# Placing the weight slabs of a four-layer trunk in the SBUF ring by a fixed order of use

## The reference, cut to what matters

```
for i in range(4):
    mod = silu(cond) @ w_ada[i] + b_ada[i]                 # 1024 x 6144: shift, scale, gate, twice
    h = rmsnorm(x) * (1 + sc1) + sh1
    y = (hyena, gla, fnet, pool)[i](h)                     # w_in, w_out / wq, wk, wv, wg, wo / fn / pool
    x = x + g1 * y
    h = rmsnorm(x) * (1 + sc2) + sh2
    # each token: the best group of four experts, in it the best two
    hid = silu(h @ w1[e]) * (h @ w3[e])                    # 1024 x 512 each
    x = x + g2 * sum_e combine[e] * (hid @ w2[e])          # 512 x 1024
y = rmsnorm(x)
```

## Time and profile before

| | before |
|---|---|
| median of 3 runs | 1425.84 us (1425.6 to 1426.71) |
| the profiled execution, whole | 1427.96 us |
| its span on the core | 1425.8 us |
| PE busy | 1277.1 us (90% of the span) |
| VectorE busy | 478.4 us (34%) |
| ScalarE busy | 278.1 us (20%) |
| read from HBM | 551.08 MB, 388 GB/s over the span |
| mean granted clock of TensorE | 0.955 |

### The profile page before, as it was taken

The page is one execution under the profiler, slowest core; times in us unless marked ns, Lnnn a source line. Parts: engine busy times, 40 slices in busy tenths (PEclk is TensorE's granted clock), DMA queues, the critical chain, the costliest instruction groups (busy, mean ns, idle before and its releaser), DMA issues.

```text
span 1425.8 us, 17690 instructions
## 1 busy us (share of the span) xinstructions
PE 1277.1 (90%) x7052; PEld 713.4 (50%) x7052; DVE 478.4 (34%) x1127; ACT 278.1 (20%) x502; POOL 32.1 (2%) x30
## 2 busy tenths in 40 slices
PE   9999999999847999999999757999997589999846
PEld 5776585444313878775444324754443245444312
DVE  3777515111103987525112102151121045111103
ACT  3311024111103221333111004331111044111101
POOL 0001310000000000010000000100000000000000
PEclk9999999999969999999999978999999799999968
DMA  9997989999999987799999999798999996999994
GB/s 385 420 417 299 402 366 406 375 429 426 428 424 421 387 362 300 276 385 391 397 427 428 428 423 420 288 413 350 430 425 427 424 422 277 397 427 427 427 425 174
DMA packets 57962, 554.41 MB, mean 389 GB/s; under 512 B 6353, under 2 KB 8337, under 8 KB 9489
## 3 DMA queue, kind: packets, MB, share of 16 engines
q1 hardware_dynamic: 56096, 551.19, 93.5%
q10 hardware_dynamic: 1778, 2.01, 0.4%
HBM read 551.08 MB, written 2.10 MB: 388 GB/s over the span
## 4 chain that ended last, share of the span: by engine, by line
PE 78%; DMA 18%; DVE 2%; ACT 1%; issue 1%; POOL 0%; SPq 0%; DVEq 0%; ACTq 0%; POOLq 0%
PE bank L797 27%; DMA ring<-in_moe_w 18%; PE bank L737 14%; PE bank L821 9%; PE bank L697 4%; PE bank L756 3%; PE bank L774 3%; PE bank L580 2%; PE bank L566 2%; PE bank L711 2%; PE bank L1052 1%; PE bank L934 1%; PE bank L647 1%; PE bank L641 1%; PE bank L984 1%; PE bank L924 1%
## 5 line engine op out<-in xcount | busy, mean ns | idle before, releaser
L797 PE MATMUL bank<-ring,arena 128*32 128x512 f32 (+1 forms) x1024 | 185.6, 663 | 92.5 <-DMA ring<-in_moe_w 92.5
L797 PE MATMUL bank<-ring,hT 128*64 128x512 f32 x1024 | 225.5, 594 | 8.6 <-DMA ring<-in_moe_w 8.6
L1572 DVE TENSOR_TENSOR rows<-rows,bank 128x512 f32<-128x512 f32 x28 | 19.3, 688 | 481.3 <-PE bank L797 481.3
L821 PE MATMUL bank<-ring,arena 128*64 128x512 f32 (+1 forms) x768 | 150.7, 642 | 18.0 <-DMA ring<-in_moe_w 17.7
L797 PEld LDWEIGHTS bank<-ring,arena 128*32 128x32 f32 (+1 forms) x1024 | 56.2, 134 | 214.6 <-issue 213.5
L797 PEld LDWEIGHTS bank<-ring,hT 128*64 128x64 f32 x1024 | 75.3, 137 | 145.9 <-issue 144.7
L737 PE MATMUL bank<-hT,ring 128*128 128x256 f32 x512 | 113.5, 381 | 0.0
L1591 DVE SCALAR_TENSOR_TENSOR yv_rest<-bank,arena,yv_big 128x512 fp32r<-128x512 f32 x56 | 42.0, 751 | 202.0 <-ACT yv_big L1250 202.0
L737 PEld LDWEIGHTS bank<-hT,ring 128*128 128x128 f32 x512 | 96.3, 190 | 18.2 <-ACT arena L1333 3.4
L821 PEld LDWEIGHTS bank<-ring,arena 128*64 128x64 f32 (+1 forms) x768 | 46.5, 135 | 108.1 <-issue 108.1
L1250 ACT ACTIVATE yv_big<-bank,arena 128x512 fp32r<-128x512 f32 x56 | 38.5, 687 | 284.1 <-PE bank L821 284.1
(11 more groups left out here) (238 smaller groups left out, 1376.6 us busy)
## 6 DMA issues: line engine op xcount, KB each, us to landing
ring<-in_moe_w SPq DMA_DIRECT2D x144, 2048.0 KB, 20.5
ring<-in_w_ada SPq DMA_DIRECT2D x96, 1024.0 KB, 11.0
ring<-in_moe_w SPq DMA_DIRECT2D x64, 1024.0 KB, 13.5
arena<-in_moe_w SPq DMA_DIRECT2D x32, 1024.0 KB, 13.7
ring<-in_hy_w_in SPq DMA_DIRECT2D x12, 1024.0 KB, 26.7
ring<-in_hy_w_out SPq DMA_DIRECT2D x4, 1024.0 KB, 10.2
ring<-in_gla_w_v SPq DMA_DIRECT2D x4, 1024.0 KB, 10.2
ring<-in_gla_w_g SPq DMA_DIRECT2D x4, 1024.0 KB, 10.8
```

The source lines that it names most:

```text
L797: last = mm(bank[4 + kind][m * o:m * o + m, :], x[:, k, at:at + m], ws[o][:, kk, :], start=k == 0, stop=k == KD - 1)
L821: last = mm(bank[6 + h][m * o:m * o + m, :], hidT[:, f, m * o:m * o + m], ws[o][:, f, :], start=f == 0, stop=f == 3)
```

## The change

The stream keeps its order. The mark `cond_done` goes. The place of a piece is now chosen by `ring_places`: `use_order` gives each piece a fixed number that stands for the time at which it is used up, and a new piece takes the place whose last piece has the lowest number (the lower place where two are equal); a couple takes the two places, even and next, whose higher number is lowest. The further rounds take places 0 to 11 by their kind and quarter. The switch `TWO_EARLY` is on and is read in `use_order` alone.

```diff
--- before.py
+++ after.py
@@ -38,6 +38,7 @@
 RING = 14
 SLAB = 2048
 SLABS = 4
+TWO_EARLY = True
 ADAS = 3 * LAYERS
 COUPLES = PAIRS // 2
 HALF = D // 8 + 1
@@ -149,10 +150,10 @@
               + wk[1:] + ada(6, 4, 6) + wv[0:1] + ada(8, 0, 2) + wv[1:2] + ada(6, 6, 7) + ada(8, 2, 4) + wv[2:3]
               + ada(6, 7) + ada(8, 4, 6) + wv[3:] + ada(7, 0, 1) + ada(8, 6) + ada(7, 1, 2) + wg[0:1] + ada(7, 2, 4)
               + wg[1:2] + ada(7, 4, 6) + wg[2:3] + ada(7, 6, 7) + wg[3:] + ada(7, 7) + ada(9) + pieces("wo", 4)
-              + ada(10) + [("cond_done", 6)],
+              + ada(10),
               pieces("fn", 4) + ada(11),
               pieces("pool", 1)]
-    out, at, held = [], 0, None
+    out = []
     for i in range(LAYERS):
         experts = [("moe", i, p, kind, q) for p in range(QUAD) for kind in range(3) for q in ((0, 2, 1, 3) if p else range(SLABS))
                    if p or kind < 2]
@@ -160,23 +161,55 @@
                     for h in range(2)]
         experts += [("moe", i, p, 2, 2 * h + e) for h in range(2) for p in (QUAD, QUAD + 1) for e in range(2)]
         for what in before[i] + experts[0:2] + [("first", i)] + experts[2:] + [("further", i)]:
-            if what[0] in ("first", "further"):
-                out.append((what, None, None))
-                continue
-            if homed(what):
-                out.append((what, None, None))
-                continue
-            if what[0] == "cond_done":
-                held = None
-                continue
-            if at % RING == held:
-                at += 1
-            if in_halves(what) and not second_half(what):
-                at += at % 2
-            if what[0] == "cond":
-                held = at % RING
-            out.append((what, at % RING, at // RING))
-            at += 1
+            out.append(what)
+    return ring_places(out)
+
+
+def use_order(what):
+
+    name, c = what[0:2]
+    if name == "moe":
+        _, i, p, kind, q = what
+        return 1000 * i + 400 + 25.7 * min(p, QUAD) + 9 * kind + 3.5 * (q // 2 + 1) + (0 if p < QUAD or kind < 2 else 0)
+    if name == "ada":
+        n, k = c, what[2]
+        if n == 0:
+            return 10 + 3.5 * k
+        if n == 1:
+            return 53 + 10 * k
+        if n == 2:
+            return 75 + 14 * k if TWO_EARLY and k < 4 else 126 + 2.5 * k
+        if n in (3, 4, 5):
+            return (146, 162, 212)[n - 3] + 2.3 * k
+        if n == 6:
+            return 1000 + (20, 25, 30, 38, 52, 55, 62, 67)[k]
+        if n == 7:
+            return 1000 + (72, 77, 82, 86, 108, 113, 118, 128)[k]
+        if n == 8:
+            return 1000 + {0: 52, 1: 53, 2: 61, 3: 62, 4: 70, 5: 71, 6: 79, 7: 80}[k]
+        if n == 9:
+            return 1000 + (142, 147, 153, 154, 160, 161, 162, 163)[k]
+        return (1192 if n == 10 else 2040) + 1.8 * k
+    return {"w_in": 47 + 7 * c, "w_out": 190 + 7 * c, "cond": 1128, "wq": 1019 + 7 * c, "wk": 1038 + 7 * c,
+            "wv": 1052 + 7 * c + (2 * c if TWO_EARLY else 0), "wg": 1000 + (80, 111, 118, 140)[c % 4], "wo": 1168 + 7 * c,
+            "fn": 2018 + 7 * c, "pool": 3010}[name]
+
+
+def ring_places(order):
+
+    free, out = [-1.0] * RING, []
+    for n, what in enumerate(order):
+        if what[0] in ("first", "further") or homed(what):
+            out.append((what, None, None))
+            continue
+        if second_half(what):
+            slot = out[-1][1] + 1
+        elif in_halves(what):
+            slot = min(range(0, RING, 2), key=lambda m: (max(free[m:m + 2]), m))
+        else:
+            slot = min(range(RING), key=lambda m: (free[m], m))
+        free[slot] = use_order(what)
+        out.append((what, slot, None))
     return out
 
 
@@ -529,7 +562,7 @@
                         for kind in range(3):
                             sp.wait_ge(s("fb_" + USED[kind]), primed(2 * (2 * (b + c) + j)))
                             for q in range(SLABS):
-                                sp.dma_start(ring[where["moe", i, 1, kind, q][0]][:],
+                                sp.dma_start(ring[SLABS * kind + q][:],
                                              expert_slab(kind, q // 2, EXPERTS * i + PAIRS * (q % 2) + j + 2 * c)) \
                                     .then_inc(s(f"fb_full{kind}"), 16)
                 for kind in range(3):
@@ -899,7 +932,7 @@
 
                         def weights(kind, h):
                             pe.wait_ge(s(f"fb_full{kind}"), 16 * SLABS * (n + 1))
-                            return [ring[where["moe", i, 1, kind, 2 * h + e][0]].rearrange("p (k n) -> p k n", k=4)
+                            return [ring[SLABS * kind + 2 * h + e].rearrange("p (k n) -> p k n", k=4)
                                     for e in range(2)]
 
                         pe.wait_ge(s(pre + "hidT_ready"), primed(n))
```

## The result

The changed kernel takes 1434.13 us (median of 5 runs, 1432.15 to 1435.18), the kernel before beside it 1426.71. The ratio is 1.0047, 95% interval [1.0032, 1.0063]: slower by 4.6 to 9.0 us. The profiled execution is the run of 1435.18 us, with a span of 1433.0.

A forecast was written before the change was run, and what follows sets the result against it. The prediction took the kernel to be bound by moving its weights over DMA. Its terms, 0 + 0.9 + 4.0 + 2.9 = 7.8 us, took the 1425.8 us span and the median to 1433.6 us, range 1429.0 to 1439.5.

The forecast's parts named there:

- Layer 0: Term for layer 0: issues move by a microsecond or two inside a full queue, gap at 262 us unchanged; 0 us.
- Retention mixer: Term for layer 1's mixer: `wv` 3 waits for `wv` 0, VectorE's 3.51 us slack covers the lateness; 0 us.
- Layer 1: Term for layer 1's expert stage: third couple waits for unit 0, seventh lands late; +0.9 us, bounds 0 and 3.4.
- Layer 2: Term for layer 2: torn second couple waits for unit 0's first quarter, less the old gap; +4.0 us, bounds 2.0 and 6.9.
- estimate of 6.8 us and 3.2: Alternative for layer 2: second couple's transfer taking 6.8 us, not 7.6, making that term 3.2 us; not used in the sum.
- Layer 3: Term for layer 3: second couple waits for unit 0's first quarter, its transfer moving behind an idle stretch; +2.9 us, bounds 2.2 and 4.9.
- grow by about the sum: Sign of being right: PE's waits on the two expert lines grow by about the summed terms, 7.8 us.
- The start: Sign of being right: PE's expert waits begin in the fifth unit of layers 2 and 3 rather than the sixth.
- the forgiving gap: Rival, not slower: late couples caught up before the second unit's gap in layers 2 and 3; 1425.8 us, chance 0.08.
- the mixer's slack: Within rival slower by more (1438.6 us, chance 0.13): VectorE's 3.51 us in layer 1's mixer fails to cover held pieces, +2.6.

The follow-up runs named there:

- e4: Kernel before, with the w1 and w3 slabs of unit 1 loaded as single slabs in order of use, not as couples: 1416.31 us, ratio 0.9924.
- e10: Kernel before, places untouched, with `wv` 3 in the retention mixer waiting for the second `wv` piece: 1430.85 us, ratio 1.0031.
- e1: Changed kernel, but both halves of a couple count as given back when the second is, in all layers: 1427.63 us, ratio 1.0007.
- e2: Changed kernel, with both halves given back together for layer 1's couples alone, which mends layer 2: 1430.61 us, ratio 1.0027.
- e3: Changed kernel, with both halves given back together for layer 2's couples alone, which mends layer 3: 1431.26 us, ratio 1.0035.
- e12: The e1 kernel run again, beside e11 on the same chip: 1426.77 us, ratio 0.9996.
- e11: Second run of the e1 kernel with two slabs of unit 0 of layer 1 exchanging places: 1431.54 us, ratio 1.0035.
- e6: Kernel before, places untouched, with layer 2's second couple waiting for the first quarter of unit 0: 1430.85 us, ratio 1.0031.
- e7: Kernel before, places untouched, with layer 2's second couple waiting for the second quarter of unit 0: 1433.62 us, ratio 1.0045.
- e8: Kernel before, places untouched, with layer 3's second couple waiting for the first quarter of unit 0: 1431.06 us, ratio 1.0026.
- e5: Kernel before, places untouched, with layer 2's second couple waiting for VectorE's first selection matrices: 1426.17 us, ratio 0.9996.

## Why the prediction was right

**Layer 0: 0.** Measured 0.4 in its loading, which runs from 206.5 to 207.0 in the other kernels but e4, with either order of places: no change that stands clear of that, as foretold.

**Retention mixer: 0, bounds 0 and 2.6.** `wv` 3 out at 504.28 (foretold 504.2), the dot for `ada` (7,1) at 519.18 (519.2), VectorE's copy 0.1 us later than before, as all of the mixer is: from its first product to unit 0 of layer 1 it takes 177.7 us in both. One thing was overlooked: a second dot waits too, 1.07 us, and the two together left 0.1 of the 3.51 us, where 0.9 was thought to be left. The term was right, its margin was not, and e10 shows what lay beyond.

**Layer 1: +0.9.** Its loading grew by 1.0, and by 0.5 to 1.0 in e1, e2, e3 and e12, which keep its late couples. But the working had two errors that cancel, and that the size fits is luck. The third couple took 8.7 us to land and not 7.7, so the seventh was 3.2 late and not 2.1; the gap gave back 2.4 and not 1.2. The fourth couple waits for unit 0 too, which the working put at nothing: behind the late third it adds nothing (it lands 4.9 us after it), but it keeps the loss when the third goes out sooner (e11). Unit 0 of layer 2 then started only 0.4 us later, as the first products of that mixer ran at the higher granted clock. This term alone was not isolated by any run.

**Layer 2: +4.0.** Measured 4.0, shown by e2 (away without the torn couple), e6 (there with one late couple alone) and e7 (its slope beyond the gap). The second couple went out at 946.87, foretold 946.5, as unit 0 began 0.4 us later than before. It landed 8.1 us after its issue, not 7.6, and the first one at 940.20: the new idle time is 954.97 - 940.20 - 4.9 = 9.9 us and not 9.6, and 5.9 came back where 5.6 was foretold, so two small errors cancel here as well. The Trainium skill ("DMA: Bandwidth & Descriptors", "Anatomy of one DMA") led to an estimate of 6.8 us and 3.2 for this layer; no run here agrees with it (e6 and e7 have 7.8 and 7.7 for this couple), and the measurement decides.

**Layer 3: +2.9.** Measured 2.8, shown by e3 and e8. The couple went out at 1205.16: the 1200.8 that was foretold, and the 4.3 us by which this layer began later.

**What failed.** PE's waits did not "grow by about the sum": 3.0 us, against 7.2 of span. The start was right: the first wait of layers 2 and 3 is in the fifth unit. But right behind a wait the granted clock was lower (0.60 from 439.67 to 445.71, against 1.00 from 966 to 976), so part of the time shows as longer work and not as waiting: PE's busy time grew by 3.8 us. In the expert stage of layer 2 its waits for a DMA grew by 0.5 us, from 30.5 to 31.0, and its busy time from 184.2 to 187.6 us, at a mean clock of 0.92 for 0.94. For the kernel before, that stage:

```profile
942.81:1157.99 215.18, 184.19 (x1020) 78.73 (x1020) 34.94 (x75) 24.37 (x38) 0.00 (x0) 0.94 0.98 413
```

That PE's clock makes no part of the loss is argued from the landings, which come late by the whole of it, and from e1, e2 and e3; around the layers the clock does move the span, by 0.8 us one way and 0.6 the other. Of the rivals, the forgiving gap was real but too short (e5, whose couple goes out 3.4 us late and still ahead of unit 0, is that rival come true), and the mixer's slack held with 0.1 us to spare.

## What to carry to other kernels

Where a stage is bound by transfers, find the last moment at which its buffers were full and the queue had to wait: in layer 2 here, lateness ahead of that moment was free up to its idle time and cost nearly its whole length beyond, and a place given back earlier there was worth as much (less in the other layers). A buffer for a double transfer comes free with the later of its halves, so fill the two halves with pieces that are used one after the other, however early one of them would be free. And where transfers set the end, compare landings, not the waits of the engine that consumes them.

## What the runs showed that had not been expected

The same last products of a layer take 5.0 to 6.5 us by the granted clock, which moves a span by over 1 us with no change in the work (e8, and e11 beside e12). A couple of 2 MB issued 0.5, 3.1 and 7.9 us behind the small router load landed 10.4, 8.7 and 7.7 us after its issue (e11, changed kernel, before); the distance was not varied by itself, so that the load is the cause is not shown.
